# Moving the second interleaved down group behind the two fifth products in each full chunk of a hybrid decoder block

## The reference

```python
D_MODEL = 2048; SEQ = 256; D_FF = 5632
def swiglu(x, wg, wu, wd):
    return (jax.nn.silu(x @ wg) * (x @ wu)) @ wd
def reference(x, ...):
    h = layer_norm(DN_ALPHA * h + 0.5 * swiglu(h, ffn1_wg[l], ffn1_wu[l], ffn1_wd[l]), ln1_g[l], ln1_b[l])
    mix = token_mixer(h, ...)
    h = layer_norm(DN_ALPHA * h + mix, ln2_g[l], ln2_b[l])
    h = layer_norm(DN_ALPHA * h + 0.5 * swiglu(h, ffn2_wg[l], ffn2_wu[l], ffn2_wd[l]), ln3_g[l], ln3_b[l])
```

## Time and profile before

| | before |
|---|---|
| median of 3 runs | 2175.01 us |
| profiled execution | 2173.46 us |
| its span, first to last instruction | 2171.7 us |
| mean granted TensorE clock | 0.995 |
| PE busy | 2136.9 us |
| DVE busy | 1734.4 us |
| ACT busy | 1310.4 us |
| loads of a weight group by SP, issue to landing, median | 7.0 us |

### The profile page before, as it was taken

One profiled execution on the slowest core, in us unless ns is written; L12 is line 12 of the kernel. 1 busy time (PEld: TensorE's weight loads), 2 busy tenths in 40 slices (PEclk: granted clock), 3 DMA queues, 4 the chain that ended last, 5 costly groups with the idle time before them and its releaser, 6 DMA issues.

```text
span 2171.7 us, 25619 instructions
## 1 busy us (share of the span) xinstructions
PE 2136.9 (98%) x9556; PEld 1771.3 (82%) x9556; DVE 1734.4 (80%) x1438; ACT 1310.4 (60%) x1303; POOL 169.9 (8%) x281
## 2 busy tenths in 40 slices
PE   8999999999999999999999999998999999999997
PEld 6888888888887888888888888886888888888886
DVE  7799999999977567677776465658899999999986
ACT  5677777777752544454545344434677777777761
POOL 0111111111010000000000000000111111101110
PEclk9999999999999999999999999999999999999999
DMA  8688888888764555555455555555678888898862
GB/s 349 233 289 273 272 268 282 264 284 298 259 242 146 203 205 172 173 185 186 153 173 192 193 196 188 217 204 203 232 233 272 269 269 293 289 301 276 291 249 85
DMA packets 97372, 508.17 MB, mean 234 GB/s; under 512 B 13440, under 2 KB 13824, under 8 KB 56704
## 3 DMA queue, kind: packets, MB, share of 16 engines
q1 hardware_dynamic: 81216, 433.50, 54.0%
q0 software_dynamic: 16064, 73.42, 15.4%
HBM read 493.23 MB, written 13.63 MB: 233 GB/s over the span
## 4 chain that ended last, share of the span: by engine, by line
PE 95%; DVE 2%; DMA 1%; ACT 0%; issue 0%; SPq 0%; POOL 0%; DVEq 0%; ACTq 0%
PE acc L1635 11%; PE acc L1634 11%; PE acc L1633 11%; PE acc L1696 11%; PE acc L1698 11%; PE acc L1697 11%; PE tb L1698 9%; PE tb L1697 9%; PE tb L1696 9%; PE tb L1681 1%; DMA g_raw<-in_groups 1%; DVE g_lo L1030 1%; DVE act_sb L1296 0%; DMA raw<-in_stream 0%; PE tb L1957 0%; PE tb L1971 0%
## 5 line engine op out<-in xcount | busy, mean ns | idle before, releaser
L1030 DVE TENSOR_TENSOR g_lo<-g_raw,g_hi 128x2048 fp32r<-128x2048 f32 x370 | 837.9, 2284 | 120.9 <-ACT g_hi L637 120.3
L637 ACT ACTIVATE g_hi<-g_raw 128x2048 fp32r<-128x2048 f32 x370 | 706.5, 1916 | 263.1 <-PE acc L1698 82.8
L1007 DVE TENSOR_TENSOR w_lo<-raw,w_hi 128x1024 fp32r<-128x1024 f32 x272 | 326.9, 1220 | 170.7 <-ACT w_hi L597 167.3
L597 ACT ACTIVATE w_hi<-raw 128x1024 fp32r<-128x1024 f32 x272 | 279.0, 1057 | 165.0 <-PE acc L1635 99.4
L1633 PE MATMUL acc<-w_hi,xT_hi 128*128 128x512 f32 x768 | 302.2, 393 | 0.0
L1635 PE MATMUL acc<-w_hi,xT_lo 128*128 128x512 f32 x768 | 299.4, 390 | 0.0
L1634 PE MATMUL acc<-w_lo,xT_hi 128*128 128x512 f32 x768 | 299.2, 390 | 0.0
L1696 PE MATMUL acc<-g_hi,xF_hi 128*128 128x512 f32 x696 | 273.3, 393 | 15.4 <-DVE g_lo L1383 9.1
L1697 PE MATMUL acc<-g_lo,xF_hi 128*128 128x512 f32 x696 | 272.0, 391 | 0.0
L1698 PE MATMUL acc<-g_hi,xF_lo 128*128 128x512 f32 x696 | 272.0, 391 | 0.0
L1696 PE MATMUL tb<-g_hi,xF_hi 128*128 128x512 f32 x568 | 221.0, 389 | 0.0
(11 more groups left out here) (148 smaller groups left out, 2866.1 us busy)
## 6 DMA issues: line engine op xcount, KB each, us to landing
g_raw<-in_groups SPq DMA_DIRECT2D x262, 1024.0 KB, 7.0
raw<-in_stream SPq DMA_DIRECT2D x272, 512.0 KB, 4.4
g_raw<-in_groups POOLq DMA_DIRECT2D x48, 1024.0 KB, 8.0
bounce<-h_sq POOLq DMA_DIRECT2D x44, 256.0 KB, 4.9
h_in<-bounce POOLq DMA_DIRECT2D x176, 64.0 KB, 2.7
ln_gb<-in_ln SPq DMA_DIRECT2D x6, 1024.0 KB, 5.3
g_raw<-in_groups SPq DMA_DIRECT2D x4, 512.0 KB, 7.6
res<-in_x_rows SPq DMA_DIRECT2D x1, 2048.0 KB, 16.4
```

Of the source, the lines that this page charges most:

```text
L597: act.activation(w_hi[:, seg.split(j)], raw[:, seg.raw(j)], ACT.Copy).then_inc(hi_ready, 1)
L637: act.activation(g_hi[:, n % RING], source[:], ACT.Copy).then_inc(g_hi_ready, 1)
L1007: dve.tensor_tensor(w_lo[:, s], raw[:, seg.raw(j)], f32(w_hi[:, s]), ALU.subtract).then_inc(lo_ready, 1)
L1030: dve.tensor_tensor(g_lo[:, n % RING], source[:], f32(g_hi[:, n % RING]), ALU.subtract).then_inc(g_lo_ready, 1)
```

## The change

In every full chunk the down group D2 is moved from directly behind D1 to behind P5b: in the numbering (`FULL`), in PE's order, and with its low part on DVE. On ACT the high part of D2 moves from behind the silu to behind that of P5b, and the seeding of its banks from before P5a to before P5b, behind the emptying of the previous chunk's D4. First and last chunks stay as they are.

```diff
-FULL = ("P1a", "P1b", "D1", "D2", "P5a", "P5b", "P6a", "P3a", "P6b", "P3b", "P7a", "P7b", "D3", "P4a", "P2a", "P2b",
+FULL = ("P1a", "P1b", "D1", "P5a", "P5b", "D2", "P6a", "P3a", "P6b", "P3b", "P7a", "P7b", "D3", "P4a", "P2a", "P2b",
         "D4", "P4b")
...
                 silu(f, b - 1)
-                split_loaded(f, b, "D2", "D2")
-                seed(f, b, "D2")
                 split_sum(f, b, "P5a", "qa", "T1a")
                 fork(f, b, Y, X, "P1b")
                 empty(f, b - 1, "D4")
+                seed(f, b, "D2")
                 act.wait_ge(t1b_ready, fulls(f, b))
                 split(f, b, "P5b", "qb")
+                split_loaded(f, b, "D2", "D2")
                 split_sum(f, b, "P6a", "qa", "T2a")
                 empty(f, b, "D1")
                 empty(f, b, "D2")
...
                 gate_rows(f, b - 1)
-                lo_group(f, b, "D2", "D2")
                 load_done(f, b, "ua")
...
                 lo_group(f, b, "P5b", "qb")
+                lo_group(f, b, "D2", "D2")
                 lo_group(f, b, "P6a", "qa")
...
                 row_group(f, b, "D1")
-                row_group(f, b, "D2")
                 wait_empty(f, b - 1, "D4")
                 product_group(f, b, "P5a", W, S1, 0, begin=True)
                 product_group(f, b, "P5b", W, S1, 1)
+                row_group(f, b, "D2")
                 wait_fork(f, b, 0)
```

## The result

The changed kernel takes 2314.29 us, the median of 4 runs (2296.98 to 2320.67), against 2175.51 us before: 1.0626 times as long, 95% interval 1.06 to 1.0653. The profiled execution took 2310.82 us with a span of 2309.0, so 137.3 us more span than before. The forecast was 2285 (2228 to 2325), slower.

What follows compares the result with a forecast made beforehand. PE was taken to bound the kernel, never waiting in a full chunk. 16 x (5.5 us hole + 1.4 us clock) = 110 us on 2173.46 gave 2283.9, and 2285 for the median, which lies 1.55 higher; range 2228 to 2325.

Steps and rivals of the forecast that it cites:

- What bounds the kernel: Full chunk: PE is busy 59.80 of 59.80 us, so reordering can't win time, only leave it alone or open a hole.
- The part costed at nothing: P5a and P5b 5.4 us earlier on PE: margins of 2.2 and 0.35 us, D2 0.9 us, so no cost.
- The floor: Before P3a: ACT's emptying, two copies and copy Z to W after D2's end leave a 2.66 us hole per full chunk.
- the rival said 2229: Rival that ub lands within 6.8 us and ACT's chain is the bound: 54 us over 16 chunks, 2229; chance 0.18.
- The load behind D2: ub, issued 9 us later, takes 9.6 us, giving a 5.5 us hole before P3a (ends 2.7 and 7.2).
- The 4.85 us from the landing to P3a: After ub lands, DVE's add, ACT's copy of P6b, its copy Z to W and wakes: P3a starts 4.85 us later.
- The sign "8 to 11 us": Expected in each full chunk of the new trace: ub lands 8 to 11 us after its issue.
- Whether the load is last: Before P3a: the load decides if it takes over 6.8 us; the rival that it isn't last had chance 0.18.
- a hole only 2.7 us long: Sign that would make the prediction wrong: holes of only 2.7 us, where 3 to 7 us was expected before P3a.
- The load that waits for both accumulations: Rival: ub lands with the second accumulation, hole before P3a 10.0 us, 182 us over 16 chunks, 2357; chance 0.12.
- The clock: Behind each hole seven matmuls run at 1.2 instead of 2.4 GHz: 1.4 us a chunk, half for a 2.7 us hole.
- The sum: Over 16 full chunks, 5.5 us of hole and 1.4 us of low clock each: 110 us, giving 2285.

Runs made afterwards that it cites:

- the causes of the hole taken away: Changed kernel with accumulating transfers cut from 1024 to 64 KB and ACT's emptying of D2 moved behind its copy Z to W: 2189.83 us.
- small accumulations: Changed kernel with the three accumulating transfers of a chunk cut from 1024 to 64 KB each: 2242.65 us.
- ub ahead of the accumulation: Changed kernel with one wait added: GpSimd issues its first accumulating transfer of a chunk only when ub has landed: 2243.98 us.
- ub into the slot of D1: Changed kernel with the loads of ub and rb exchanged, ub into D1's slot and rb into D2's: 2245.41 us.
- the moved emptying: Changed kernel with ACT's emptying of D2 moved from before P3a's high part to behind the copy Z to W: 2276.4 us, run again 2310.78 us.
- the late load alone: Kernel before, order untouched, with ub issued only when the low part of P5b is written: 2264.37 us, second run 2309.25 us.
- half the way: Changed kernel with D2 behind P5a instead of behind P5b on all engines: 2185.49 us, 1.0042 times the kernel before.

## Why the prediction was right

**What bounds the kernel** held. PE had no idle time in a full chunk to win back, and everything that any engine was late by before P3a became time.

**The part costed at nothing** held: PE's new order with P5a, P5b and D2 early shows no hole at these groups in any chunk, and with the causes of the hole taken away the kernel is 15 us from the one before, nearly all of it at the short waits that are left before P3a.

**The floor** held to 0.02 us: 2.66 forecast, 2.68 in the trace, and 5.18 us for ACT's chain. As the bound of a whole kernel it gave 2242.65 to 2245.41 in three experiments where the rival said 2229. In the trace with small accumulations, 15 us above that, 9 of them are the clock (20.4 us behind its 16 holes, where half of 1.4 us a chunk had given 11), 2.6 the ends of the records before the holes, and 2.8 lie outside the full chunks.

**The load behind D2** held in mechanism, and its size is the larger of the two misses. The forecast took 9.6 us, the middle between two D3 loads. The 16 loads of ub took 6.0 to 12.4 us, 10.6 in the mean and eight of them more than the 11.3 that was forecast as the slow end. In these chunks most of the first accumulation goes ahead of ub and the second runs beside it (see below); the D3 loads of the rows had at most the end of the first beside them. With that the mean hole was 98.9 / 16 = 6.2 us instead of 5.5, 11 us over the 16 chunks. The 4.85 us from the landing to P3a was 543.59 - 538.81 = 4.78 from the add that the landing released. The sign "8 to 11 us" held for the mean and for four of the 16 loads.

**Whether the load is last** is decided by a race, which the prediction named as a rival of its own and priced as if a whole kernel went one way. It is drawn chunk by chunk: three fast ones and 13 slower ones in this execution, other numbers in others. It would explain why the changed kernel spreads over 2287.81 to 2320.67 us in its eight runs, 33 us, where the kernel before keeps within 6; only two of the eight have a trace. By the prediction's own sign, a hole only 2.7 us long, it was wrong in two chunks of the first trace and in three of the second.

There was luck in it. The chunk of the rows is the one of its 14 like it (all but the first of each feed-forward) in which GpSimd issued the accumulation earliest, 14.5 us behind the chunk's start; in the others it was 14.6 to 16.9, and with ub at 15.25 the load would have come first in nearly all. What kept them slow is that in the changed kernel the accumulation is issued earlier, at 12.9 to 15.2 us, as the prediction argued against this rival from the bounce transfers, without a number.

**The load that waits for both accumulations** (hole 10.0) didn't happen; the longest was 8.05. Over 527 to 530, with ub issued at 526.4, the DMA engines moved the accumulation alone (first row below); over 530 to 533 both queues moved the same 0.39 MB (second and third row). q0 is GpSimd's queue, q1 SyncE's; packets, MB, share of the engines' time.

```profile
q0 software_dynamic: 63, 0.52, 87.1%
```

```profile
q0 software_dynamic: 48, 0.39, 67.2%
q1 hardware_dynamic: 48, 0.39, 32.3%
```

The first piece of ub starts 3.98 us after its issue, when 80 of the accumulation's pieces of 8 KB (the view counts them as packets) have started. Where no large accumulation is near, with small ones, it starts after 0.95 us. So there is a wait first, of some 3 us, and then an equal share of bytes, at about 0.32 us for a piece of the load and 0.63 for one of the accumulation. The rule of the Trainium skill, "DMA: Bandwidth & Descriptors", section "Queues, rings and completion order", that a whole packet of one ring is drained before the next ring's turn, fits the wait of some 3 us, if at all. In the stretch after it the pieces start 16 of one queue, then 16 of the other, so the turns are short, and the measured share decides.

**The clock** held in kind and was too small in size: 1.4 us a chunk were taken from the hole of 6.26 us, read as seven matmuls at the low level; counted over the changed kernel's trace, matmuls more than 0.25 us apart behind each hole, the loss was 1.6 to 2.9 us, 33.1 in all or 2.1 a chunk. Eight to fourteen matmuls were slow, not seven. That is 11 us more. The other long wait of the earlier trace rows, of only 3.16 us, warned of it: behind its matmul at 682.93 the low level lasted until 688.51, over 5 us, as these rows of the kernel before show:

```profile
688.08 0.63 PE L1635 MATMUL acc<-w_hi,xT_lo 128*128 128x512 f32 x1
688.51 0.45 PE L1633 MATMUL acc<-w_hi,xT_hi 128*128 128x512 f32 x1
688.79 0.40 PE L1634 MATMUL acc<-w_lo,xT_hi 128*128 128x512 f32 x1
```

**The sum again:** 98.9 us idle and 33.1 us of low clock are 132 of the 137.3 us of span. The idle time is counted from the end of a record of 0.39 us, where the next matmul was due after 0.227, which adds 16 x 0.16 = 2.6. Of the 2.8 us left 2.4 lie outside the full chunks, 2.1 of them ahead of the first one, and were not followed.

**What was not settled.** Why the accumulation is ahead in one chunk and not in the next can be followed one step back. In the chunk that starts at 511.10 GpSimd sends the hidden rows out, brings them back and issues the accumulation at 525.03 (above):

```profile
515.03 1.13 POOL L1588 DMA_DIRECT2D bounce<-h_sq  x2 [6.65 <-DVE h_sq L1067]
520.28 3.85 POOL L1596 DMA_DIRECT2D h_in<-bounce  x7 [4.12 <-DMA bounce<-h_sq]
```

In all chunks but the first of each feed-forward the second of the two bounce transfers is issued 4.50 us behind the chunk's start and ub 15.25, and the accumulation 4.3 to 4.7 us behind the bounce transfer's landing. In the changed kernel's first trace the transfer landed after 4.0 to 6.3 us: where it took 5.6 us or less the accumulation won, where it took 5.9 or more ub did. Why 256 KB take so different times stays open, and no run held them fixed.

## What to carry to other kernels

When work moves later on the bounding engine, list what waits for its end and for its inputs' release, with the queue behind each: here two waits that nobody had moved, an emptying on ScalarE and a load into a freed slot, made nearly all of the loss. A load that is issued just in time is only as good as what stands in the DMA queues beside it, so read its landing time with the heaviest neighbour in front of it, and take the slow end. If a hole can't be avoided keep it under 2 us: the clock then stayed up in every case here, and above 2.6 us it mostly cost another 1.7 us.

## What the runs showed of the hardware

**The price of a hole on the clock.** Of 48 holes of 2.67 or 2.68 us in three of the experiments (small accumulations, ub ahead of the accumulation, ub into the slot of D1) 38 were followed by matmuls 0.43 us apart, which is 1.2 in place of 2.4 GHz, at a loss of 1.4 to 1.7 us, once 3.0, and ten by none. In the two traces of the changed kernel two of five such holes were. Of the 18 holes of 1.2 to 2.0 us before P3a or D3, in all traces, none was, and of four of 2.0 to 2.3 us one. The time at the low level may begin up to 1.5 us after the matmuls have started again, as in this row of the kernel with ub in D1's slot, of which the sixth matmul behind it was the first slow one:

```profile
392.73 0.47 PE L1696 MATMUL acc<-g_hi,xF_hi 128*128 128x512 f32 x1 [2.68 <-DVE g_lo L1030]
```

**A plain load behind an accumulating one.** The late load of ub, 1024 KB from HBM, took 4.7 to 6.5 us beside small accumulations or ahead of full ones (once 7.7, with the accumulation issued 0.1 us behind it), and 9.2 to 13.0 us when an accumulation of the same size was issued 1 us or more before it with a second one to follow. A lead of 1 us of one queue over another doubled the time of a transfer.

**What decides the race.** The first piece of an accumulation starts 1.6 to 1.8 us after its issue where it is first, and that of a plain load with only small accumulations near 0.95. By these two the accumulation is first if it is issued more than 0.7 us ahead (my estimate from these figures). All 96 chunks of the six traces with a late load and full accumulations agree (the changed kernel twice, the moved emptying twice, the late load alone, half the way): with a lead of 0.61 us or less the load's first piece started first, with 0.70 or more the accumulation's did. Where the load was first, the accumulation's first piece came up to 4.9 us after its issue.
